# Experts' tokens gathered one chunk at a time, with the one-hots stationary, in a fused three-block transformer kernel

## What is computed

```python
def hier_moe(tokens, w1, b1, w2, b2, w_gate, w_up, w_down):
    p1 = softmax(tokens @ w1 + b1)                 # 4 groups
    p_grp, grp = lax.top_k(p1, 1)
    lg2 = (tokens @ w2 + b2).reshape(n, 4, 8)      # 8 experts per group
    top_val, top_idx = lax.top_k(lg2 of the group, 2)
    gate = p_grp * softmax(top_val)
    expert = grp * 8 + top_idx
    return grouped_experts(tokens, expert, gate, w_gate, w_up, w_down)

def run(args):                                     # for each block of an expert's tokens
    xb, e = args
    return (silu(xb @ w_gate[e]) * (xb @ w_up[e])) @ w_down[e]
```

## Time and profile before

| | us |
|---|---|
| median of 3 runs | 2038.86 (2032.32 to 2039.28) |
| the profiled execution, its own time | 2040.79 |
| its span, first to last instruction | 2039.0 |
| TensorE busy | 1824.0 (89%) |
| VectorE busy | 972.0 (48%) |
| ScalarE busy | 556.2 (27%) |
| GpSimd busy | 566.3 (28%) |

### The profile page before, as it was taken

How to read it: one execution, slowest core, us unless ns; L and a number is a source line. 1 busy time by engine, 2 the same in 40 slices (tenths; PEclk the granted TensorE clock), 3 DMA queues, 4 the chain that set the end, 5 groups by cost and what they waited for, 6 DMA issues and landing times.

```text
span 2039.0 us, 55781 instructions
## 1 busy us (share of the span) xinstructions
PE 1824.0 (89%) x22868; PEld 1303.2 (64%) x22869; DVE 972.0 (48%) x2272; ACT 556.2 (27%) x1099; POOL 566.3 (28%) x431
## 2 busy tenths in 40 slices
PE   7999979999999998898988986666668999999998
PEld 4444466666666665554676764545447677788887
DVE  3797164666666666455444532222336995210001
ACT  2001243333333333214433422122223314210000
POOL 0000025666666663001014432222239000100000
PEclk9999989999999998999989988888888999999999
DMA  9854166889999999932059999999996356443320
GB/s 368 312 194 165 42 254 270 363 340 425 425 425 423 427 425 406 334 117 73 1 222 416 408 428 428 430 428 428 430 417 245 124 185 229 146 143 117 131 104 21
DMA packets 109380, 574.34 MB, mean 282 GB/s; under 512 B 4976, under 2 KB 10224, under 8 KB 84592
## 3 DMA queue, kind: packets, MB, share of 16 engines
q1 hardware_dynamic: 108720, 570.72, 70.0%
q10 hardware_dynamic: 576, 2.43, 0.3%
HBM read 572.08 MB, written 1.05 MB: 281 GB/s over the span
## 4 chain that ended last, share of the span: by engine, by line
PE 69%; DMA 19%; DVE 7%; issue 3%; SPq 2%; ACT 2%; DVEq 0%
PE bank L352 24%; PE bank L560 18%; DMA ring<-in_expert_w_down 13%; PE bank L532 6%; PE bank L511 6%; PE bank L982 4%; DMA ring<-in_expert_w_gate 2%; PE bank L609 2%; DVE b L1042 2%; ACT b L1862 1%; DMA ring<-in_conv_w_in 1%; PE bank L898 1%; PE bank L423 1%; DMA ring<-in_attn_w_in 1%; DMA ring<-in_expert_w_up 1%
## 5 line engine op out<-in xcount | busy, mean ns | idle before, releaser
L560 PE MATMUL bank<-ring,b 128*32 128x128 f32 (+1 forms) x13600 | 527.7, 308 | 119.4 <-issue 50.4
L560 PEld LDWEIGHTS bank<-ring,b 128*32 128x32 f32 x13600 | 397.7, 115 | 304.3 <-issue 210.1
L1042 DVE TENSOR_TENSOR h_t<-h_t,bank 128x512 f32<-128x512 f32 (+1 forms) x696 | 350.6, 566 | 446.5 <-PE bank L532 446.5
L1862 ACT ACTIVATE b<-bank 128x256 f32<-128x256 f32 (+6 forms) x464 | 178.4, 397 | 1157.9 <-PE bank L352 398.0
L352 PE MATMUL bank<-h_t,ring 128*128 128x256 f32 (+1 forms) x1600 | 427.8, 430 | 4.9 <-ACT h_t L1862 2.5
L352 PEld LDWEIGHTS bank<-h_t,ring 128*128 128x128 f32 x1600 | 309.6, 194 | 117.0 <-issue 77.1
L2308 POOL TENSOR_SCALAR b<-b 128x1024 f32<-128x1024 f32 (+1 forms) x85 | 195.2, 2297 | 58.7 <-POOL b L2316 33.6
L2316 POOL TENSOR_TENSOR b<-b 128x512 f32<-128x512 f32 (+1 forms) x85 | 89.3, 1051 | 421.6 <-PE bank L532 421.6
L532 PE MATMUL bank<-b 32*128 32x512 f32 (+1 forms) x1392 | 172.9, 568 | 5.4 <-DVE h_t L1042 4.7
L2311 POOL TENSOR_TENSOR b<-b,b 128x1024 f32<-128x1024 f32 (+1 forms) x85 | 161.4, 1899 | 7.1
L1042 DVE TENSOR_TENSOR b<-b,bank 128x128 f32<-128x128 f32 (+3 forms) x124 | 49.8, 406 | 200.7 <-PE bank L352 155.0
(11 more groups left out here) (298 smaller groups left out, 1510.0 us busy)
## 6 DMA issues: line engine op xcount, KB each, us to landing
ring<-in_expert_w_gate SPq DMA_DIRECT2D x64, 2048.0 KB, 13.7
ring<-in_expert_w_up SPq DMA_DIRECT2D x64, 2048.0 KB, 15.9
ring<-in_expert_w_down SPq DMA_DIRECT2D x64, 2048.0 KB, 16.0
ring<-in_ada_w SPq DMA_DIRECT2D x24, 2048.0 KB, 15.4
ring<-in_w_mod SPq DMA_DIRECT2D x12, 2048.0 KB, 8.5
ring<-in_w_in SPq DMA_DIRECT2D x6, 2048.0 KB, 10.5
ring<-in_w_ffn_gate SPq DMA_DIRECT2D x5, 2048.0 KB, 7.7
ring<-in_w_ffn_up SPq DMA_DIRECT2D x5, 2048.0 KB, 7.8
```

Source lines behind the costliest of these rows:

```text
L560: last = pe.matmul(b[32 * m:32 * m + 32, 0:width], lhs[:, k, :], rhs[:, k, m * width:(m + 1) * width], start=(k == 0), stop=(k == nk - 1), ...
L1042: return dv.tensor_tensor(o, a, b, op)
L1862: return ac.activation(o, i, f, **kw)
```

## The change

The dispatch handles one chunk, the next one, instead of a quarter of a block of four. The stationary operand is the chunk's one-hot (128 tokens x 32 slots, one per token tile), the moving one the token rows, 256 features in each of four column groups. The result in bank 3 has slots down the partitions, and VectorE turns it in 32x32 blocks straight into `xe` (`turn_slots`). For this ScalarE stores the token rows `h_tok` in another order of columns. The one-hot of one chunk is made by three VectorE operations: a compare of slot numbers 0 to 31 with both slots of every token, the sum of the two results, and a subtraction of 32 from the slots, for the next chunk. The slot table, `h_q`, `xe_wide` and the three ScalarE copies are gone; one dispatch instead of four stands ahead of the loop. The register loads of the loop bounds, ahead of gate before, now stand between up and dispatch.

```diff
-                def dispatch(b, part, buf):
-                    for kk in range(2):
-                        for t in range(tiles):
-                            last = pe.matmul(b[:, kk * P:(kk + 1) * P], part(t, kk),
-                                             b3[:, bass.ds(disp_at + t * P + buf, P)],
-                                             start=(t == 0), stop=(t == tiles - 1))
-                    last.then_inc(s["xq_full"], 1)
-                pe.wait_ge(s["disp_ready"], 8)
-                for q in range(4):
-                    dispatch(bank[q], lambda t, kk: h_tok[:, t, (2 * q + kk) * P:(2 * q + kk + 1) * P], 0)
+                def dispatch(n):
+                    pe.wait_ge(s["disp_ready"], n + 1)
+                    for t in range(tiles):
+                        for m in range(4):
+                            last = pe.matmul(bank[3][32 * m:32 * m + 32, 0:256], one_hot[:, 32 * t:32 * t + 32],
+                                             h_tok[:, t, 256 * m:256 * m + 256],
+                                             start=(t == 0), stop=(t == tiles - 1), tile_position=(0, 32 * m))
+                    last.then_inc(s["xs_full"], 1)
+                dispatch(0)
...
                             pe.wait_ge(s["xe_taken"], n + 1)
+                            four_lanes(bank[0], xe, wg, KD, P).then_inc(s["gate_full"], 1)
+                            combine(n, 0)
+                            expert_loaded(1)
+                            four_lanes(bank[1], xe, wu, KD, P).then_inc(s["up_full"], 1)
                             if j == 0:
                                 pe.reg_load(bound[2], cum[0:1, bass.ds(e + 2, 1)])
                             else:
                                 pe.reg_load(bound[0], cum[0:1, bass.ds(e + 1, 1)])
                                 pe.reg_load(bound[1], cum[0:1, bass.ds(e + 2, 1)])
-                            four_lanes(bank[0], xe, wg, KD, P).then_inc(s["gate_full"], 1)
-                            combine(n, 0)
-                            expert_loaded(1)
-                            four_lanes(bank[1], xe, wu, KD, P).then_inc(s["up_full"], 1)
-                            pe.wait_ge(s["disp_ready"], n * 2 + 16)
-                            pe.wait_ge(s["xq_taken"], n + 4)
-                            pe.wait_ge(s["hq_ready"], n + 1)
-                            dispatch(bank[3], lambda t, kk: v3(h_q, 0, 4, 256)[:, t, kk * P:(kk + 1) * P], ((n + 4) % 8 // 4) * (tiles * P))
+                            dispatch(n + 1)
                             combine(n, 1)
...
+                own, both = picks[:, :, 0:tiles], v4(picked, 0, 2, tiles, CAP)
...
+                def place_tokens(n):
+                    dv.wait_ge(s["picked"], n * 2 + 1)
+                    tt(both, cn("iota", 0, CAP).unsqueeze(1).unsqueeze(1).broadcast_to([P, 2, tiles, CAP]),
+                       own.unsqueeze(3).broadcast_to([P, 2, tiles, CAP]), ALU.is_equal).then_inc(s["picked"], 1)
+                    dv.wait_ge(s["picked"], n * 2 + 2)
+                    tt(one_hot[:, 0:tiles * CAP], picked[:, 0:tiles * CAP], picked[:, tiles * CAP:2 * tiles * CAP], ALU.add) \
                         .then_inc(s["disp_ready"], 1)
+                    tt(own, own, caps[:, :, 0:tiles], ALU.subtract).then_inc(s["picked"], 1)
+                def turn_slots(n):
+                    dv.wait_ge(s["xs_full"], n + 1)
+                    dv.transpose(xe.rearrange("p k s -> p (k s)"), bank[3][:, 0:256]).then_inc(s["xe_taken"], 1)
+                place_tokens(0)
+                turn_slots(0)
+                place_tokens(1)
...
                     dv.transpose(hid_t, hid).then_inc(s["hid_ready"], 1)
-                    place_tokens(n + AHEAD, (n % 8) * width)
+                    turn_slots(n + 1)
+                    place_tokens(n + 2)
                     add_parts(n, 1)
...
                     act(silu_g, bank[0][:, 0:P], ACT.Silu).then_inc(s["gate_taken"], 1)
-                    take_quarter(n + 4, bank[3], ((n + 4) % 8) * 256)
-                    take_xe(n + 1, (n + 1) % 8 // 4, (n + 1) % 4)
-                    take_h((n + 1) % 4)
                     ac.wait_ge(s["y_full"], n + 1)
```

More of the change, by code:

```diff
@@ L244, in two_blocks @@
         spread = v3(b3, 0, 4, 512)
-        disp_at = 2048
+        picked, one_hot = b3[:, 2048:2304], b3[:, 2304:2432]
         silu_g, hid, hid_t = [b3[:, 3072 + P * i:3200 + P * i] for i in range(3)]
-        slot_a, slot_b = [b3[:, 3456 + 80 * i:3536 + 80 * i] for i in range(2)]
-        h_q = b3[:, 3616:4640]
+        picks, caps = v3(b3, 3456, 2, 4), v3(b3, 3464, 2, 4)
         diag = [b12[:, 6656:7168], b12[:, 7168:7680], b3[:, 3616:4128], b3[:, 4128:4640]]
@@ L1123, in moe @@
                 done()
[L1124 removed]
+                step(dv.memset(caps, float(CAP)))
                 step(dv.memset(nch[1], 1.0))
@@ L1226, in moe @@
                 dv.sem_inc(sem(f"placed{layer}"), 1)
-                s = {k: sem(f"{k}{layer}") for k in ("disp_ready", "gate_taken", "up_full", "hid_made", "hid_ready", "part_full",
-                                                      "part_added")}
-                width = tiles * 32
-                blocks = MOST // 4 + AHEAD // 4
-                def slot_table(first, last):
-                    if tiles == 4:
-                        for out, slots in ((slot_a, g[0]), (slot_b, g[1])):
-                            step(tt(v3(out, 4 * first, last - first, 4), fl(slots).unsqueeze(1).broadcast_to([P, last - first, 4]),
-                                    chunk_base[:, 2 * first:2 * last:2].unsqueeze(2).broadcast_to([P, last - first, 4]),
-                                    ALU.subtract))
-                    else:
-                        for t in range(2):
-                            for out, slots in ((slot_a, g[0]), (slot_b, g[1])):
-                                step(tt(v4(out, 4 * first, last - first, 2, 2)[:, :, t, :],
-                                        slots[:, t, :].unsqueeze(1).broadcast_to([P, last - first, 2]),
-                                        v3(chunk_base, 2 * first, last - first, 2), ALU.subtract))
-                    done()
@@ L1256, in moe @@
-                slot_table(0, 1)
-                for n in range(4):
-                    place_tokens(n, n * width)
-                slot_table(1, blocks)
-                for n in range(4, AHEAD):
-                    place_tokens(n, n * width)
+                s = {k: sem(f"{k}{layer}") for k in ("picked", "disp_ready", "xs_full", "xe_taken", "gate_taken", "up_full", "hid_made",
+                                                      "hid_ready", "part_full", "part_added")}
+                own, both = picks[:, :, 0:tiles], v4(picked, 0, 2, tiles, CAP)
@@ L1943, in moe @@
                     b, t, half = full(), i // 2, i % 2
-                    rows = h_tok[:, t, :].rearrange("p (k q) -> p q k", k=KD)
-                    taken(act(rows[:, 64 * half:64 * half + 64, :], b.rearrange("p (q k) -> p q k", k=KD), ACT.Copy))
+                    rows = h_tok[:, t, 512 * half:512 * half + 512].rearrange("p (m k q) -> p m q k", m=2, k=KD)
+                    taken(act(rows, b.rearrange("p (m q k) -> p m q k", m=2, k=KD), ACT.Copy))
                 ac.wait_ge(a_free, taken.n)
@@ L1969, in moe @@
                     take_turned(pieces[2][-1])
[L1970 to L1990 removed]
+                s = {k: sem(f"{k}{layer}") for k in ("gate_full", "gate_taken", "y_full", "y_taken")}
                 for i in range(4):
```

36 lines of the change are left out of this document (6 added, 30 removed).

## The result

The changed kernel takes 2019.27 us (median of 5 runs, 2015.04 to 2020.76), the kernel before on the same chip 2037.33 (2032.32 to 2039.28): a ratio of 0.9913, 95% interval 0.9902 to 0.9924. It is faster by 18 us, or 0.87%. The prediction said 2040, no change as the likeliest, with a range down to 2019. What came is its first rival, "the subtraction slips through", which it put at 2022 with a chance of 0.33.

A forecast was written before the change was run, and what follows sets the result against it. It took TensorE to bound layer 0, within 1% of the weights' limit, and the weights layer 1. Terms of +13, -9.3, -1.8 and -2 gave 0, carried through +2, +1 taken: 2040 us, range 2019 to 2056.

The forecast's parts named there:

- first rival: VectorE's subtraction isn't held by GpSimd: TensorE's period 9.6 us, weights limit layer 0's gain to 14 to 16; 2022, chance 0.33.
- What bounds the kernel: Layer 0 is paced by TensorE, within 1% of the weights' limit; layer 1, from about its fifteenth chunk, by the weights.
- The dispatch on TensorE: In the loop, four column groups side by side take 1.7 us instead of 1.98, saving 0.28 us a chunk.
- The register loads: Between up and dispatch, one load hides and two stick out by 0.3 us, so 0.2 us a chunk in layer 0.
- The rival in which they lose all cover: Register loads behind up cost 0.9 instead of 0.2 us and delay VectorE: period 10.8, about 2068, chance 0.10.
- VectorE's chain: Turn, compare, sum, subtraction and adds run in series behind the dispatch; unheld, adds end at S+4.18, before TensorE's S+4.7.
- S: Start of the second combine, which is the end of the dispatch's slot; times in the loop count from it in us.
- GpSimd is in the way: GpSimd's sum from S+1.34 holds VectorE's subtraction to S+2.65 to 2.85; adds end S+5.15 to 5.35, period 10.16 us.
- Ahead of the loops: Shorter dispatch before each loop: layer 0's gate 9.3 us earlier; layer 1 2.9 earlier, 2 counted, bounds 0 to 3.
- The end of layer 0: Gate and up of the last experts wait for weights, some 1.8 us more than usual; a slower loop removes it.
- The sum: Whole kernel: +13, -9.3, -1.8, -2 gives 0, carried through +2, +1 taken, so 2040 against the median of 2038.86.
- the main case: In layer 0's loop GpSimd holds VectorE's subtraction: period 10.16 us, 0.28 longer; 2040, own range 2030 to 2052, chance 0.55.

The follow-up runs named there:

- late_two: The changed kernel with two idle 128x128 VectorE transposes between the turn and the sum over the places; 2035.30 us.
- late_three: The changed kernel with three idle 128x128 VectorE transposes between the turn and the sum over the places; 2038.56 us.
- late_turn: The changed kernel with one idle 128x128 VectorE transpose between the turn and the sum over the places; 2019.11 us.
- prelude0: The changed kernel with the 32 matmuls of layer 0's first dispatch issued four times over; 2023.54 us.
- before_short: The kernel before with the dispatch ahead of each layer's loop made over the first block of tokens only; 2028.62 us against 2037.68.
- prelude1: The changed kernel with the 16 matmuls of layer 1's first dispatch issued four times over; 2022.59 us.

## Why the prediction came out as it did, step by step

**What bounds the kernel.** Right: 424 against 428 GB/s said that layer 0 has next to no room beyond 450 us, and the runs show it (4.8 us, or up to 6.9 by the other kernels with the same loop, where TensorE alone would give 11.2). The three parts of the first rival's layer 0 were 9.3, 4 and 3, cut to 14 to 16; measured 9.5 and 4.8, so 14.3.

**The dispatch on TensorE.** 1.7 predicted, 1.73 in the chain. Side by side, as down.

**The register loads.** 0.3 us behind up in odd experts predicted; the two kinds of period are 9.36 and 9.80, so 0.43 with two loads. The mechanism was right, with the cover put a little too large; that one load hides came out too. The rival in which they lose all cover didn't come. That the dispatch hides them altogether, the prediction didn't see.

**VectorE's chain: the step that failed.** The subtraction was put at S+1.54 and it starts at S+1.13. Four small terms, all with the same sign, make the 0.41 us. The turn starts at S+0.13, not 0.25: I took the start of ScalarE's copy behind the old dispatch for that of VectorE's turn behind the new one. It isn't a matter of the engine. In the same trace ScalarE's SiLU starts 0.13 us behind the next slot, when what it reads comes from gate, which has four column groups as the new dispatch has:

```profile
448.04 0.71 PE L532 MATMUL bank<-b 32*128 32x512 f32 x4
448.17 0.28 ACT L1862 ACTIVATE b<-bank 128x128 f32<-128x128 f32 x1 [0.37 <-PE bank L560]
```

Why it is 0.25 us behind the old dispatch, no run tells. From the turn's start to the compare's 0.38 instead of 0.44, since records overlap. From the compare to the sum 0.41 instead of 0.42 + 0.14: the gap of 0.14 between two dependent operations stands behind an operation of 0.29 us; behind this one of 0.38 it is 0.03. From the sum to the subtraction 0.21 instead of 0.29: these two don't depend on one another, and overlap by 0.08. The turn out of PSUM takes 0.45, as predicted (0.44). Each term was inside its bounds or had none given; the bounds of the start, 0.12 earlier here and 0.15 there, were not summed up for the one number that decides, the distance from GpSimd's start. It was called 0.2 us behind, it is 0.21 ahead.

**GpSimd is in the way.** The mechanism is right and its size too, as late_two and late_three show: held to GpSimd's end, adds to S+5.15, period 10.19, 16 us. (The total that went with it, 2040, is 5 us over late_two's 2035.30.) In the changed kernel it just isn't reached: the subtraction starts 0.21 us ahead of GpSimd, late_turn's 0.01 ahead was still free, and the nearest held start lies 0.17 behind, so the margin is between 0.20 and 0.38 us. The rule read at 297 us, that the operation begun 0.05 us ahead goes through and the one behind it doesn't, held in every kernel. The Trainium skill's page SBUF — State Buffer, section SBUF: two separate sides, states it as a lock of the pair of ports shared by VectorE and GpSimd, got by whichever starts first and kept for the whole instruction; late_two agrees, with a sum that runs its 0.29 us across GpSimd's start, a GpSimd operation that grows by 0.11 us, and a subtraction that takes 1.24.

The rival gave two reasons. One was that GpSimd's recorded span might be off; nothing here needs that. The other was that the distance stood on a computed turn, "and 0.2 us less would do". That is what happened, only that not the turn's length but its start and the spacings behind it were shorter, by 0.41 us in all. So the rival was right in kind, and its chance of 0.33 was set too low for a distance that small.

**Ahead of the loops.** Layer 0: 9.3 predicted, 9.5 measured, and prelude0 and before_short show that most of such a saving arrives. Layer 1: 2 predicted with 0 to 3 as bounds, 2.8 measured for a first gate that comes 3.7 us earlier behind the first dispatch (2.93 us instead of 6.65). The argument, that the stream is almost gapless there and only its idle time can be won, stands: before, it moves 391 GB/s from 1063.7 to 1071.0, ahead of the first gate. What it left out is that the stream can lose as well, as prelude1 shows.

**The end of layer 0.** "With a slower loop that wait goes": in late_two, the slower loop, TensorE waits for weights once, 0.64 us at 787.51. With the faster one the waits grow, to 3.04 us at 765.36.

**The sum.** Put the measured loop into it: replace the term of +13 for 47 x 0.28 by the loop's measured -4.8, leave out the 1.8, which is in it: 2040.8 - 4.8 - 9.3 - 2 = 2024.7, or some 2023 against the median, near the first rival's 2022. 2019.27 came, and the 2.3 us that the trace has between the layers (more likely the loop's), with the 0.8 more of layer 1, are most of what is left. The chance of 0.55 for the main case rested on 0.2 us of computed distance, with an error that turned out twice that. That the time still lies inside the stated range is owed to the second case, for which the range was stretched down to 2019. Even odds would have been fairer, and the better forecast would have named the distance as the uncertain number.

## What to carry to other kernels

Where two engines exclude each other, the order of their starts decides, and a tenth of a microsecond can be worth all of the gain: sum up the uncertainty of that distance, and take its terms from start-to-start spacings on the same engine, not from lengths laid end to end. Slack doesn't protect a chain that has such a lock in it; put the operations with two SBUF inputs ahead of the other engine's start with room to spare, or behind it. And when a stage is within 1% of a second limit, count what is saved ahead of the stage nearly whole where the second limit's stream waits for the stage to start (layer 0 here), and what is saved inside it by that limit.

## What the runs showed of the hardware

- VectorE held by a tensor-tensor operation of GpSimd waits to its end: 8 elements took 1.24 us instead of 0.16, 128 took 1.26 instead of 0.29. The compare with one input in the constants' tile, 128x256, went through in 0.38 us when it started ahead. The adds with one input in PSUM are not held: none of some 350 in layer 0 took over 0.69 us, in the changed kernel and in late_two.
- GpSimd's 128x512 sum has a record of 1.29 us, and of 1.40 where a VectorE sum of 0.29 us starts 0.02 us ahead of it.
- A start 0.01 us ahead of GpSimd's recorded start was free, one 0.17 us behind was not; the durations are the same in all 43 to 46 chunks of a kernel.
- An idle transpose of 128x128 with nothing depending on it has a record of 0.27 us (0.31 for the hidden layer's) and moves what follows by 0.20 us, each of three by 0.19.
- A transpose of 128x256 float32 out of PSUM takes 0.45 us, against 0.31 for 128x128 inside SBUF.
- The dispatch in four column groups, 32 records with 256 columns, adds 1.73 us to the chain at the full clock; two register loads behind up show as 0.43 us, one as nothing, and two behind the dispatch as nothing.
